# A ring of four instead of eight buffers for gathered expert v rows

## The chip, the cores and the metric

One core of a Trainium2 chip runs the whole program. The metric is the device time of one execution in microseconds. The kernel before took 5160.54 us (median of three runs, 5151.05 to 5163.83). TensorE is called PE here, VectorE DVE, ScalarE ACT, GpSimd POOL and SyncE SP, as in the profile.

## The reference, cut to what matters

Two layers of a diffusion backbone work on 5 blocks of 128 tokens with 1024 channels. Each layer has attention and pooling, and then the part that this case is about, a mixer that fetches expert rows by key:

```
def one_block(xb):                        # 128 tokens
    q = (xb @ wq).reshape(n, 8, 2, 64)
    s = einsum('nhpk,pmk->nhpm', q, sub_keys)
    sv, si = top_k(s, 16)                 # best 16 of 128 keys, on both sides
    ...                                   # best 16 of the 256 pairs: expert numbers e, gates g
    act = gelu(einsum('nd,nhkd->nhk', xb, u[e]))
    return einsum('nhk,nhkd->nd', g * act, v[e])
```

So every token has 8 heads with 16 experts each, and every expert costs one row of `u` and one row of `v`, each 1024 float32 numbers (4 KB). For the 128 tokens of a block one such step is a transfer of 512 KB.

## The kernel before

Five engines run lists of instructions written out by hand, with semaphores between them. A layer has two stages: attention with its projections, and the expert stage, which takes about 72% of the span.

The expert stage runs over *units*. A unit is one block (5) and one head (8): 40 units in a layer, 80 in all; they are counted from 0 to 79 here (`unit` in the code), and rows within a unit from 0 to 15. u5 of a unit is its sixth u row, v4 its fifth v row. For each unit:

- DVE finds the 16 experts of every token (`topk`, in short steps put between other work, two units ahead).
- POOL issues one indirect DMA for each row (`gather`, L578; POOL runs the list in order). Its loop takes, for k from 0 to 15, row k of u of the *next* unit and then row k of v of *this* unit. Before an issue it waits until the buffer is free: `used >= row - n + 1`, n being the number of buffers of the ring. The u ring has 4 buffers (`URING`), the v ring 8 (`RING`).
- DVE takes the dot product of each u row with the tokens (L1221, in the order of landing). A second instruction reads the sum out and frees the buffer.
- When all 16 are done, ACT applies gelu (L830). DVE multiplies by the gates (`weights`, L1194), but only behind the dot product of row 0 of the next unit. ACT then makes 16 diagonal matrices of the weights (L837).
- PE multiplies each diagonal with its v row and adds it up in PSUM (`v_rows`, L1564; four matmul records for each row, two halves of 512 columns in two passes). The last of them frees the v buffer (`v_used`).

PE and ACT do other things between the v rows of two units. `BESIDE` puts, behind the v rows of units 0 to 4 of each layer, queries for later blocks and gate rows there (L1533, L812). Before the v rows of the last unit of a block, PE also turns the tokens of the next block (`peer_tokens`, L1555), and before each unit it computes scores (L1549). At a block's end ACT copies the sum (L851) and DVE adds it to the tokens.

The tile `PR` is used twice. In the attention stage it holds queries, keys and values (13312 floats for each partition); in the expert stage it holds the v ring from its start, and behind the ring the queries `pq_T`.

Of the kernel before, what the change touches and what calls it, by code (L numbers as in the profile page):

```python
# [15 lines left out]
P = 128  # L16
D = 1024
KC = D // P
LAYERS = 2
NB = 5  # L20
# [12 lines left out]
PH, NKEYS, TOPK = 8, 128, 16  # L33
NEXP = NKEYS * NKEYS
NEG = -1e30
URING, RING = 4, 8
SPAN = 3 * STRIP
RB = (2 * WIN_R - 1) * (2 * WIN_C - 1)
RB_PAD = 64
# [85 lines left out]
def build(nc, x_prompt, x_sample, c, c_ctx, cache_nat_k, cache_nat_v, cache_mla_ckv, cache_mla_krope,  # L125
# [6 lines left out]
    with ExitStack() as ctx:  # L132
        def sb(name, free, dt=f32, parts=P):
            return ctx.enter_context(nc.sbuf_tensor(name, [parts, free], dt))
# [10 lines left out]
        HO = sb("h_or_mixed", NB * D)  # L145
        WR = sb("weight_ring", SLOTS * KC * 512)
        QKN = sb("na_qk_or_gates", 3 * NB * P + 3 * NKB * P)
        PR = sb("mla_qkv_or_expert_rows", RING * D + PH * NB * P)
        SC = sb("scratch", 4608)
        GB = sb("bias_or_small_weights", 2304)  # L150
        rows = sb("vec_rows", P)
# [45 lines left out]
        o = 0  # L197
        qm_T = PR[0:QK, o:o + HEADS * NB * P].rearrange("p (h t) -> p h t", h=HEADS)
        o += HEADS * NB * P
        km_T = PR[0:QK, o:o + HEADS * NKB * P].rearrange("p (h t) -> p h t", h=HEADS)  # L200
        o += HEADS * NKB * P
        v_mla = PR[:, o:o + NKB * WIDTH].rearrange("p (b h e) -> p b h e", b=NKB, h=HEADS)
        o += NKB * WIDTH
        v_na = PR[:, o:o + NKB * WIDTH].rearrange("p (b n) -> p b n", b=NKB)
        o += NKB * WIDTH
        mod_rows = PR[0:2, 0:2 * 512].rearrange("p (s n) -> p s n", s=2)
        lat_T = PR[:, o:o + 256].rearrange("p (k t) -> p k t", k=2)
        v_ring = [PR[:, i * D:(i + 1) * D] for i in range(RING)]
# [1462 lines left out]
```

## Time and profile before

| | |
|---|---|
| median of three runs | 5160.54 us |
| the profiled execution | 5150.62 us, its span 5148.8 us |
| PE busy | 3930.9 us (76%) |
| POOL busy | 2554.3 us (50%) |
| DVE busy | 2559.4 us (50%) |
| ACT busy | 946.7 us (18%) |
| gathers | 2560, with 1342 MB of the 1448 MB that are moved |
| granted PE clock, mean | 0.926 |

The page of the profile gives the busy time of each engine, a strip of the span in 40 slices, a chain of work that ended last, and groups of instructions. The expert stages are slices 6 to 20 and 26 to 40, where the DMA engines are busy for nine tenths. POOL's busy time is the making of the gathers; the time in which the data moves is in the DMA rows.

### The profile page before, as it was taken

To read this page: it belongs to the slowest core of one execution; us is meant where nothing else is said; L and a number is where in the kernel's file an instruction comes from. 1 tells how busy PE (TensorE), PEld (TensorE's weight loads), DVE (VectorE), ACT (ScalarE), POOL (GpSimd) and SP (SyncE) were. 2 spreads that over 40 slices of the span, in tenths; PEclk is the share of its full clock that TensorE was granted. 3 is DMA by queue.
4 is the path that set the end of the run, shared out by engine and by line. 5 is a ranking of instruction groups with operands and counts; after the bars stand their busy time and mean duration, and the time that the engine had idled before them with its cause. 6 is when DMAs were issued, how large, how long until landed. Compare 5 with 4: busy or idle time off the path is not lost. (4 is left out here: it accounts for less than half of the span.)

```text
span 5148.8 us, 36114 instructions
## 1 busy us (share of the span) xinstructions
PE 3930.9 (76%) x10138; PEld 1745.8 (34%) x10138; DVE 2559.4 (50%) x6404; ACT 946.7 (18%) x2474; POOL 2554.3 (50%) x2831
## 2 busy tenths in 40 slices
PE   7889958777777677777788898688776777776777
PEld 3467333322222222222244664333222222222222
DVE  1243155455665556565422431555656565565563
ACT  1132112111111111111111321111111111111111
POOL 1210045566666666666612000455666666666665
PEclk9985989999999999999999859899999999999999
DMA  4110268899999999999930102688999999999998
GB/s 160 40 59 17 98 244 306 324 389 363 374 359 366 362 369 364 364 370 364 368 109 35 59 33 98 237 329 322 371 369 366 363 367 369 364 370 359 373 367 332
DMA packets 435149, 1448.27 MB, mean 281 GB/s; under 512 B 59236, under 2 KB 69768, under 8 KB 434440
## 3 DMA queue, kind: packets, MB, share of 16 engines
q0 software_dynamic: 368640, 1342.34, 68.7%
q1 hardware_dynamic: 66312, 103.61, 5.9%
q8 instruction: 86, 1.41, 0.1%
q14 instruction: 111, 0.91, 0.0%
HBM read 1442.20 MB, written 3.57 MB: 281 GB/s over the span
## 5 line engine op out<-in xcount | busy, mean ns | idle before, releaser
L1564 PE MATMUL scores<-mla_qkv_or_expert_rows,weight_diagonals 128*128 128x512 f32 x5120 | 2574.6, 634 | 1039.3 <-DMA mla_qkv_or_expert_rows<-in_peer_v,experts 587.6
L1564 PEld LDWEIGHTS scores<-mla_qkv_or_expert_rows,weight_diagonals 128*128 128x128 f32 x5120 | 925.7, 197 | 2653.5 <-issue 2436.2
L578 POOL DMA_INDIRECT mla_qkv_or_expert_rows<-in_peer_v,experts x1280 | 1209.5, 945 | 642.6 <-issue 368.7
L1221 DVE CUSTOM_DVE_ANT_0 bias_or_small_weights<-bias_or_small_weights,scores_transposes 128x1024 f32<-128x1024 f32 x640 | 779.3, 1218 | 529.2 <-DMA bias_or_small_weights<-in_peer_u,experts 443.6
L1221 DVE CUSTOM_DVE_ANT_0 na_qk_or_gates<-na_qk_or_gates,scores_transposes 128x1024 f32<-128x1024 f32 x640 | 779.5, 1218 | 475.7 <-DMA na_qk_or_gates<-in_peer_u,experts 332.1
L578 POOL DMA_INDIRECT na_qk_or_gates<-in_peer_u,experts x640 | 604.2, 944 | 535.8 <-DVE dots L1221 257.3
L578 POOL DMA_INDIRECT bias_or_small_weights<-in_peer_u,experts x640 | 608.9, 951 | 253.3 <-issue 173.9
L521 POOL TENSOR_SCALAR stat_biased<-stat_sums 128x6 f32<-128x6 f32 (+1 forms) x82 | 16.3, 199 | 1107.0 <-ACT scratch L607 823.0
L837 ACT ACTIVATE weight_diagonals<-ident,expert_weights 128x128 f32<-128x128 f32 x1280 | 386.7, 389 | 306.4 <-DVE expert_weights L1194 112.4
L1342 PE MATMUL products<-weight_ring,h_or_mixed 128*128 128x384 f32 (+2 forms) x800 | 266.4, 494 | 0.0
L819 ACT ACTIVATE scratch<-scratch 128x16 f32<-128x16 f32 x80 | 24.7, 308 | 1245.4 <-issue 550.8
L1262 PE MATMUL scores_transposes<-ident,scratch 128*128 128x128 f32 (+1 forms) x814 | 166.0, 340 | 100.0 <-POOL scratch L544 34.9
L830 ACT ACTIVATE gelu_dots<-dots 128x16 f32<-128x16 f32 x80 | 17.3, 217 | 1064.7 <-issue 671.6
L1342 PEld LDWEIGHTS products<-weight_ring,h_or_mixed 128*128 128x128 f32 x800 | 153.7, 206 | 99.6 <-issue 43.7
L1262 PEld LDWEIGHTS scores_transposes<-ident,scratch 128*128 128x128 f32 (+1 forms) x814 | 116.8, 169 | 145.6 <-issue 58.0
L1289 PE MATMUL products<-weight_ring,silu_cond 128*2 128x512 f32 x320 | 147.1, 617 | 11.4 <-DMA weight_ring<-in_w_mod 11.4
L939 DVE COPY scratch<-scores_transposes 128x256 f32<-128x256 f32 x80 | 33.7, 422 | 233.2 <-remote 191.5
L1485 PE MATMUL products<-mla_qkv_or_expert_rows,scratch 128*128 128x64 f32 x864 | 147.1, 327 | 0.0
L1533 PE MATMUL products<-h_or_mixed,weight_ring 128*128 128x128 f32 (+1 forms) x512 | 144.1, 444 | 3.3 <-issue 3.3
L1485 PEld LDWEIGHTS products<-mla_qkv_or_expert_rows,scratch 128*128 128x128 f32 x864 | 145.6, 252 | 0.5 <-issue 0.4
L1517 PE MATMUL products<-weight_ring,scratch 128*128 128x512 f32 x320 | 144.4, 611 | 0.0
L1221 DVE DVE_READ_ACCUMULATOR2_ANT dots<- 128x1 f32 x1280 | 106.8, 83 | 0.6 <-issue 0.6
(176 smaller groups left out, 2712.5 us busy)
## 6 DMA issues: line engine op xcount, KB each, us to landing
weight_ring<-in_w_mod SPq DMA_DIRECT2D x24, 2048.0 KB, 8.6
mla_qkv_or_expert_rows<-in_peer_v,experts POOLq DMA_INDIRECT x1280
na_qk_or_gates<-in_peer_u,experts POOLq DMA_INDIRECT x640
bias_or_small_weights<-in_peer_u,experts POOLq DMA_INDIRECT x640
weight_ring<-in_w_in SPq DMA_DIRECT2D x6, 1536.0 KB, 6.9
weight_ring<-in_t_pool SPq DMA_DIRECT2D x4, 2048.0 KB, 7.6
weight_ring<-in_w_out SPq DMA_DIRECT2D x4, 2048.0 KB, 7.8
weight_ring<-in_peer_wq SPq DMA_DIRECT2D x4, 2048.0 KB, 8.0
```

The source lines that it names most:

```text
L578: g.indirect_dma_start(ring[row % n], None, table, bass.IndirectOffsetOnAxis(ap=idx_st[:, col:col + 1], axis=0),).then_inc(row_in[row % n] ...
L819: a_.activation(tk["ex"], tk["tv"], ACT.Exp, bias=tk["nmx"], accum_out=tk["sum"]).then_inc(gexp_ready, 1)
L837: a_.activation(diags[:, k * P:(k + 1) * P], ident[:, :], ACT.Copy, scale=wgt[:, w:w + 1]).then_inc(diag_ready, 1)
L939: v_.tensor_copy(tk["scores"], key_scores(unit)).then_inc(score_free, 1)
L1221: v_.tensor_tensor_reduce(out=u_ring[at % URING], in0=u_ring[at % URING], in1=tokens, scale=1.0, scalar=0.0, op0=ALU.mult, op1=ALU.add, ac ...
L1262: ins = t_.transpose(dst[0:n, j * P:(j + 1) * P], v, ident[:, :])
L1289: ins = t_.matmul(dst[0:2, :], sct[:, :].rearrange("p (c k) -> p k c", c=2)[:, kk, :], w[:, kk, :], start=kk == 0, stop=kk == KC - 1)
L1342: ins = t_.matmul(dst[:, 0:n], hT(b, kk), w[:, kk, 0:n], start=kk == 0, stop=kk == KC - 1)
L1485: ins = t_.matmul(dst[:, h * DH:(h + 1) * DH], prob_T[(i - 2) % 2][:, k, :], val, start=k == 0, stop=k == len(blocks) - 1)
L1517: ins = t_.matmul(dst, o_T[ots.slot((l, b))][:, kk, :], w[:, kk, :], start=kk == 0, stop=kk == KC - 1)
L1533: ins = t_.matmul(dst[:, 0:(b1 - b0) * P], w[:, kk, (h % 4) * P:(h % 4 + 1) * P], h_blocks[:, b0:b1, kk, :], start=kk == 0, stop=kk == KC - 1)
L1564: ins = t_.matmul(acc[:, hf * 512:(hf + 1) * 512], diags[:, k * P:(k + 1) * P], v_ring[at % RING][:, hf * 512:(hf + 1) * 512], start=n % P ...
```

## The change

The ring of v rows gets four buffers. The constant `RING` sets the number of buffers, of semaphores `v_row_in`, and the distance of POOL's wait: gather of v row r now waits until row r-4 has been used, not r-8. The ring of u rows and the order of the gathers stay. The tile `PR` keeps its 13312 floats; the queries `pq_T` now begin behind four rows instead of eight, and as the view takes all of the rest of the tile, the queries of two heads lie 1152 floats apart instead of 640.

```
-URING, RING = 4, 8
+URING, RING = 4, 4
...
-        PR = sb("mla_qkv_or_expert_rows", RING * D + PH * NB * P)
+        PR = sb("mla_qkv_or_expert_rows", 13312)
```

## Rows read from the trace of the kernel before

**Rows 1.** The page: DMA strip, rate of its 40 slices, chain by engine.

```profile
DMA  4110268899999999999930102688999999999998
GB/s 160 40 59 17 98 244 306 324 389 363 374 359 366 362 369 364 364 370 364 368 109 35 59 33 98 237 329 322 371 369 366 363 367 369 364 370 359 373 367 332
...
PE 13%; POOL 12%; issue 8%; DMA 7%; another core or an unknown queue 3%; DVE 2%; ACT 0%; DVEq 0%; POOLq 0%; ACTq 0%
```

**Rows 2.** The page's groups: busy us, mean ns, idle before and what ended it.

```profile
L1564 PE MATMUL scores<-mla_qkv_or_expert_rows,weight_diagonals 128*128 128x512 f32 x5120 | 2574.6, 634 | 1039.3 <-DMA mla_qkv_or_expert_rows<-in_peer_v,experts 587.6
...
L578 POOL DMA_INDIRECT mla_qkv_or_expert_rows<-in_peer_v,experts x1280 | 1209.5, 945 | 642.6 <-issue 368.7
```

**Rows 3.** POOL, timeline, unit 20: start, us, [idle before, releaser]; v2, v3, v4.

```profile
1691.58 0.94 POOL L578 DMA_INDIRECT mla_qkv_or_expert_rows<-in_peer_v,experts  x1 [4.79 <-remote]
...
1694.07 0.94 POOL L578 DMA_INDIRECT mla_qkv_or_expert_rows<-in_peer_v,experts  x1 [0.30 <-issue]
...
1696.55 0.94 POOL L578 DMA_INDIRECT mla_qkv_or_expert_rows<-in_peer_v,experts  x1 [0.30 <-issue]
```

**Rows 4.** PE, timeline, unit 20: v0 with v1, then v2, v3, v4.

```profile
1691.80 3.70 PE L1564 MATMUL scores<-mla_qkv_or_expert_rows,weight_diagonals 128*128 128x512 f32 x8 [2.99 <-ACT weight_diagonals L837]
1696.11 1.96 PE L1564 MATMUL scores<-mla_qkv_or_expert_rows,weight_diagonals 128*128 128x512 f32 x4 [0.61 <-DMA mla_qkv_or_expert_rows<-in_peer_v,experts]
1699.93 1.95 PE L1564 MATMUL scores<-mla_qkv_or_expert_rows,weight_diagonals 128*128 128x512 f32 x4 [1.87 <-DMA mla_qkv_or_expert_rows<-in_peer_v,experts]
1703.01 1.96 PE L1564 MATMUL scores<-mla_qkv_or_expert_rows,weight_diagonals 128*128 128x512 f32 x4 [1.13 <-DMA mla_qkv_or_expert_rows<-in_peer_v,experts]
```

**Rows 5.** Waits of POOL, whole span: us in total, times, longest.

```profile
POOL na_qk_or_gates L578 <- DVE dots L1221: 257.3, 81, 13.1
```

**Rows 6.** POOL, timeline, unit 2: v0, v4, then u5 of the next unit.

```profile
816.06 0.94 POOL L578 DMA_INDIRECT mla_qkv_or_expert_rows<-in_peer_v,experts  x1 [2.06 <-remote]
...
826.03 0.94 POOL L578 DMA_INDIRECT mla_qkv_or_expert_rows<-in_peer_v,experts  x1 [0.30 <-issue]
837.08 0.94 POOL L578 DMA_INDIRECT na_qk_or_gates<-in_peer_u,experts  x1 [10.11 <-DVE dots L1221]
```

**Rows 7.** PE, timeline, unit 2: the queries before it, its first v rows.

```profile
818.99 13.90 PE L1533 MATMUL products<-h_or_mixed,weight_ring 128*128 128x512 f32 x32
...
835.82 14.41 PE L1564 MATMUL scores<-mla_qkv_or_expert_rows,weight_diagonals 128*128 128x512 f32 x29 [2.50 <-ACT weight_diagonals L837]
```

**Rows 8.** L1564 in stretches: PE and PEld busy (instructions), clock, DMA share, GB/s.

```profile
1100.30:1104.12 3.82, 3.81 (x5) 1.74 (x6) 0.50 0.93 341
835.80:838.79 2.99, 2.97 (x5) 1.38 (x6) 0.65 1.05 408
...
2430.80:2434.45 3.65, 3.65 (x5) 1.70 (x6) 0.54 0.58 173
3454.20:3457.52 3.32, 3.31 (x5) 1.50 (x6) 0.58 0.14 19
```

**Rows 9.** POOL, timeline, unit 43: v4, then u5 of the next unit.

```profile
3443.22 0.94 POOL L578 DMA_INDIRECT mla_qkv_or_expert_rows<-in_peer_v,experts  x1 [0.30 <-issue]
3455.46 0.94 POOL L578 DMA_INDIRECT na_qk_or_gates<-in_peer_u,experts  x1 [11.30 <-DVE dots L1221]
```

**Rows 10.** PE, timeline, unit 43: its first v rows.

```profile
3454.21 10.12 PE L1564 MATMUL scores<-mla_qkv_or_expert_rows,weight_diagonals 128*128 128x512 f32 x19 [2.50 <-ACT weight_diagonals L837]
```

**Rows 11.** POOL, timeline, unit 7: v4.

```profile
1101.25 0.94 POOL L578 DMA_INDIRECT mla_qkv_or_expert_rows<-in_peer_v,experts  x1 [0.30 <-issue]
```

**Rows 12.** POOL, timeline, unit 36: v4.

```profile
2433.10 0.94 POOL L578 DMA_INDIRECT mla_qkv_or_expert_rows<-in_peer_v,experts  x1 [0.30 <-issue]
```

**Rows 13.** All engines in two stretches: us, PE, PEld, DVE, ACT, POOL, clock, DMA, GB/s.

```profile
680.00:1060.00 380.00, 279.69 (x598) 111.57 (x596) 202.83 (x551) 62.54 (x160) 207.73 (x220) 0.91 0.86 322
1060.00:2560.00 1500.00, 1082.24 (x2193) 394.89 (x2194) 890.53 (x2264) 256.78 (x673) 988.71 (x1047) 0.96 0.96 367
```

**Rows 14.** PE, timeline, unit 79: v4 to v15.

```profile
5121.29 20.84 PE L1564 MATMUL scores<-mla_qkv_or_expert_rows,weight_diagonals 128*128 128x512 f32 x48 [0.73 <-DMA mla_qkv_or_expert_rows<-in_peer_v,experts]
```

## The prediction, made before the changed kernel was run

> **What bounds the kernel now.** I read the page first. Its DMA strip and rates show the two expert stages, flat at about 365 GB/s with the DMA engines nine tenths busy; the chain that ended last names no single engine, but mostly PE, POOL and DMA [rows 1]. The change touches only the v rows, so the groups come next: PE spends 2574.6 us on 1280 v rows, 2.01 us each, and stood idle for 587.6 us because a v row had not landed; making a gather costs POOL 0.945 us [rows 2].
>
> The pace is in the timelines. POOL issues one gather in 1.245 us (0.94 of work, 0.30 of gap): v3 at 1694.07 and v4 at 1696.55 have one u gather between them, so a pair of u and v takes 2.49 us [rows 3]. PE needs 1.96 us of these for a v row, and it waits for the DMA before v2, v3 and v4 [rows 4]. So within a unit POOL's list sets the pace, and whatever holds POOL up holds up both rings. Three things hold it: pauses of 2 to 5 us every 28 gathers or so, which the trace puts down to no engine (4.79 us before v2, [rows 3]; I count 94, of 3.8 us); the u ring (257.3 us in 81 waits on one of its two tiles, the longest 13.1 us, [rows 5]); and, in no case, the v ring: going through all 1280 v gathers, none was issued less than 3.3 us after the row eight before it was used.
>
> So the question is by how much a ring of four would have bound. I set each issue of v row r beside the end of PE's fourth matmul on row r-4, and split what I found by the place in the unit.
>
> **Within a unit: nothing.** v4 of unit 20 is issued at 1696.55 and PE starts on it at 1703.01, 6.46 us later, because of the DMA [rows 3, 4]. With 1.96 us of matmuls and the 0.3 us that POOL takes to go on, a buffer is taken for 8.7 us. Four buffers allow one row every 8.7 / 4 = 2.2 us, and POOL asks for one every 2.49 us. The margin is 9.96 - 8.7 = 1.2 us. Cost 0, if the landing doesn't take longer than now. That it would take less, with fewer gathers under way, seems more likely, since a stall lets the queue run empty.
>
> **At the start of a unit: four kinds.** v4 waits for v0, and v0 can't be used before the unit's gelu, weights and first diagonal are there. In unit 20 v0 and v1 are done at 1695.5, v0 alone about 1693.8, and v4 went out at 1696.55 [rows 3, 4]: covered, by POOL's pause.
>
> (a) Behind the work of `BESIDE`, 10 units (1 to 5 and 41 to 45). PE computes queries for 13.90 us, and unit 2's v0 starts only at 835.82 [rows 7]; its four matmuls end at about 838.8 [rows 8]. v4 had gone out at 826.03 [rows 6], so it would be 13 us late. But POOL stood still anyway: the next gather, u5, came at 837.08 after 10.11 us of waiting for DVE [rows 6]. What counts is how much later u5 comes: 838.8 + 0.27 for v4, + 1.25 for u5 = 840.3, 3.2 us later. Unit 43 the same way: v0 starts at 3454.21 and ends at about 3457.5, u5 at 3455.46, so 3457.5 + 1.52 - 3455.46 = 3.6 us [rows 8 to 10]. The ten lie between 1.8 and 3.8 us and sum to 29 us. The stall is longer than any queue of gathers, so nothing hides it: 29 us on the path.
>
> (b) The last unit of a block, 7 units (7, 15, 23, 31, 55, 63, 71). Here PE turns the next block's tokens first. In unit 7 v0 starts at 1100.30 and ends near 1104.1, as PE has just stood idle and its four matmuls run at a granted clock of 0.50, which is 1.2 GHz [rows 8]. v4 was issued at 1101.25 [rows 11]: 1104.1 + 0.27 - 1101.25 = 3.1 us late. The seven sum to 22 us.
>
> (c) 22 other units in which v0 is late by chance, such as unit 36: v0 ends at 2434.4, v4 was issued at 2433.10, 1.6 us late [rows 8, 12]. Between 0.1 and 2.7 us each, 16 us in all. In the 39 units left over (the last of each layer is apart, below), a ring of four would not have been waited for.
>
> (d) The last unit of each layer has no u gathers. PE alone sets its end: it takes v4 to v15 in 20.84 us, 1.74 us each [rows 14], so four rows in 7.0 us. With a ring of four, a buffer turns round in 0.3 + 1.96 us and the time from issue to PE's start: 4.53 us for v2 of unit 20, which was issued after a pause, or 6.46 us for v4 [rows 3, 4]. That is 6.8 or 8.7 us, and costs twelve rows 0 or 12 x 1.7 / 4 = 5 us. Few gathers are under way there, so I stay near the lower end: 1.5 us in each layer, 3 us.
>
> A stall in (b) and (c) begins with about five gathers under way (6.46 us at 1.245), and the DMA works on. After a pause a v row needs 4.53 us, two rows later 6.46 us [rows 3, 4], so up to 1.9 us of a stall can be hidden at first; but as the latency grows back within some gathers, a part is paid after all. I take half: 19 us of 38. Bounds: 38 with nothing hidden, 0 with all of it.
>
> The rest has one answer. `pq_T` with 1152 floats between heads has the same operands of each instruction in form, so ACT L812 and PE L1549 cost what they did; four semaphores fewer cost or give nothing; `PR` is as large. No DMA is added or moved past another. Behind POOL's new wait stand only gathers, first u5 of the next unit, for which DVE waits. A gain could come only from rows that land sooner once fewer are under way; the sum leaves it out, and I bound it at 10 us, one microsecond in each unit of (a).
>
> **Sum.** 29 + 19 + 3 = 51 us. The profiled execution took 5150.62 us, 9.9 below the median of 5160.54. So 5202 for an execution like the profiled one, and 5160.5 + 51 = 5211.5 against the median, which I predict as 5211.
>
> **The rivals.**
>
> *The stalls are hidden (not slower).* If the DMA, not POOL, set the pace over a longer stretch, then POOL's pauses would be its slack: what the v ring delays, the next pause would give back. Place: POOL's pauses, 94 of 3.8 us; it decides if a pause shrinks by what came late before. Then (b) and (c) are 0, and (a) keeps a part, 0 to 20 us: 5160 to 5180, typically 5165. For it: 9 tenths of DMA share. Against it: the stretch with the BESIDE units moves 322 GB/s and the rest 367 [rows 13]; a stall isn't made up for there, and the pauses are as frequent in it. The Trainium skill bears on this rival (HBM Reference, Specifications): it gives a core about 358 GB/s as its share, and says that one that streams alone measures more. By the share alone the gathers' 1342 MB would take 3750 us, about the length of both stages, and the change would cost nothing; the 367 GB/s of [rows 13] are above it, and so the trace disagrees with the share as a limit here.
>
> *The ring binds in every pair (much slower).* If the landing takes over 1.2 us longer than the 6.46 us, each pair costs (cycle)/4 and not 2.49 us. At 0.1 us for each of 1280 pairs that is 128 us more: 5340. For it: the margin is thin, and next-layer weights under way beside gathers lengthen landings. Against it: a ring that stalls has fewer rows under way, and these land sooner.
>
> *Faster.* Four rows fewer under way shorten the wait for u rows at the start of a unit, by up to 0.3 us in each of 80 units or 24 us, and the stalls are hidden too: 5140. Nothing in the trace shows it.
>
> **Chances.** Forecast (25 to 90 us later) 0.70; hidden 0.14; binding in every pair 0.12; faster 0.04. A difference below 0.3%, 15.5 us, can't be told from none. Of the hidden case three quarters fall within it: faster 0.03, same 0.13, slower 0.84. The range takes in the full 70 us and some of the two neighbours: 5168 to 5270.
>
> **What would show it.** In the profile after, POOL should wait for PE before v4 in some 35 to 40 units; in the ten BESIDE units the wait of 10 us moves from u5 (on DVE) to v4 (on PE), and u5 follows 1.25 us behind v4. POOL's waits for DVE fall by about 100 us and those for PE rise by 150. Within units the pace stays 2.49 us. PE's and DVE's busy time stay the same within 1%. The rate falls by 1% in the flat slices. I am wrong if v8 to v15 wait for PE in many units (the ring binds), or if POOL's pauses got shorter or fewer (hidden).

## The result

The changed kernel took 5208.16 us (median of four runs, 5202.75 to 5214.84) against 5159.91 us: 48 us more, a ratio of 1.0097 with a 95% interval of 1.0079 to 1.0114. I had said 5211 us, 51 us more. The profiled execution is the slowest of the four, 5214.84 us with a span of 5213.0 us; 64 us more than the profiled one of before.

The page of the kernel after, with the lines that answer to [rows 1, 2]:

```profile
DMA  4110267799999999999931102677999999999998
GB/s 158 40 58 33 97 230 283 300 372 368 367 341 370 373 352 368 373 349 369 367 125 40 58 33 97 230 290 298 367 369 372 365 368 368 361 372 368 373 368 323
...
L1564 PE MATMUL scores<-mla_qkv_or_expert_rows,weight_diagonals 128*128 128x512 f32 x5120 | 2572.3, 631 | 1108.5 <-DMA mla_qkv_or_expert_rows<-in_peer_v,experts 753.2
...
L578 POOL DMA_INDIRECT mla_qkv_or_expert_rows<-in_peer_v,experts x1280 | 1209.1, 945 | 999.1 <-PE scores L1564 411.1
```

The work is what it was (2572.3 us of PE for the v rows, 1209.1 us of POOL for their gathers). POOL's idle time before v gathers rose from 642.6 to 999.1 us, and the largest part of it is now put down to PE. The loss is not even over the stage: slices 7 and 8 fell from 306 and 324 GB/s to 283 and 300, slices 27 and 28 from 329 and 322 to 290 and 298, while the flat slices of the second layer are mostly within 1%; in the first layer slices 9, 12, 15 and 18 lost 4 to 6% as well. The same in stretches (columns as in [rows 13]):

```profile
680.00:1060.00 380.00, 269.02 (x564) 105.94 (x563) 191.22 (x517) 56.33 (x142) 194.31 (x207) 0.90 0.80 297
1060.00:2560.00 1500.00, 1059.55 (x2166) 382.58 (x2165) 885.75 (x2261) 260.42 (x688) 978.12 (x1034) 0.97 0.96 364
```

322 GB/s became 297 in the stretch with the BESIDE units, 8% less; 367 became 364 in the rest, 1% less. POOL's waits answer to [rows 5] (us in total, times, longest):

```profile
POOL mla_qkv_or_expert_rows L578 <- PE scores L1564: 411.1, 178, 19.1
...
POOL na_qk_or_gates L578 <- DVE dots L1221: 54.2, 51, 7.8
```

The wait for DVE on this u tile went from 257.3 to 54.2 us. (Most of the 143.9 us that the profile of before puts down to PE for v rows are pauses that it can't name: set beside the end of the matmuls, POOL waited 0.6 us for v buffers before and 241 us after.) The wait moved from the u ring to the v ring, as forecast, but it got longer than forecast. The timeline of POOL in unit 3 shows how; first the kernel before (v0, then u5 of the next unit), then the kernel after (v0, v4, u5, v13):

```profile
871.04 0.95 POOL L578 DMA_INDIRECT mla_qkv_or_expert_rows<-in_peer_v,experts  x1 [5.64 <-issue]
...
891.62 0.94 POOL L578 DMA_INDIRECT na_qk_or_gates<-in_peer_u,experts  x1 [9.67 <-DVE dots L1221]
```

```profile
877.62 0.95 POOL L578 DMA_INDIRECT mla_qkv_or_expert_rows<-in_peer_v,experts  x1 [0.30 <-issue]
...
906.41 0.94 POOL L578 DMA_INDIRECT mla_qkv_or_expert_rows<-in_peer_v,experts  x1 [19.13 <-PE scores L1564]
907.66 0.94 POOL L578 DMA_INDIRECT na_qk_or_gates<-in_peer_u,experts  x1 [0.30 <-DVE dots L1221]
...
931.88 0.94 POOL L578 DMA_INDIRECT mla_qkv_or_expert_rows<-in_peer_v,experts  x1 [3.38 <-remote]
```

Before, POOL's unexplained pause (5.64 us) fell ahead of the wait for the queries. It cost nothing there: without it POOL would have come to u5 earlier and waited longer. After, the pause (3.38 us) falls on v13, behind the wait, where all that follows is late. I summed this over the ten units behind BESIDE work, from every gather of both traces. Pauses ahead of the long wait were 31.6 us before and 5.3 us after, pauses behind it 2.0 us before and 28.3 us after. The ten units took 546.4 us from v0 to the next v0 before and 604.3 us after, 58 us more; the seven last units of blocks 338.9 and 341.3 us; 59 others 2690.4 and 2694.8 us.

So the total came out as forecast, but not its parts: 29 us had been given to the ten units, which lost 58, and 19 to the others, which lost 7. Part of the agreement is luck. One pair of traces can't tell whether this split is the mechanism or chance, and that was the question of the experiments. Several kernels of them keep eight buffers and shorten only the distance of POOL's wait, so that the place of the stall can be chosen.

### The profile page after: what moved, and what is told of

It reads as the page before. It is cut to its first block and busy times, and to the rows that moved or that the text cites. A ratio compares the mean times of both kernels' runs of the same rounds, so it can differ in the third digit from the quotient of the medians.

```text
span 5213.0 us, 36114 instructions
## 1 busy us (share of the span) xinstructions
PE 3927.5 (75%) x10138; PEld 1729.6 (33%) x10138; DVE 2569.2 (49%) x6404; ACT 942.1 (18%) x2474; POOL 2557.1 (49%) x2831
## 5 line engine op out<-in xcount | busy, mean ns | idle before, releaser
L1564 PE MATMUL scores<-mla_qkv_or_expert_rows,weight_diagonals 128*128 128x512 f32 x5120 | 2572.3, 631 | 1108.5 <-DMA mla_qkv_or_expert_rows<-in_peer_v,experts 753.2
L1564 PEld LDWEIGHTS scores<-mla_qkv_or_expert_rows,weight_diagonals 128*128 128x128 f32 x5120 | 910.7, 196 | 2736.5 <-issue 2543.0
L578 POOL DMA_INDIRECT mla_qkv_or_expert_rows<-in_peer_v,experts x1280 | 1209.1, 945 | 999.1 <-PE scores L1564 411.1
L1194 DVE TENSOR_TENSOR expert_weights<-gelu_dots,gates 128x16 f32<-128x16 f32 x80 | 13.8, 173 | 184.2 <-ACT gelu_dots L830 168.6
```

The costliest lines, as they stand in the source:

```text
L578: g.indirect_dma_start(ring[row % n], None, table, bass.IndirectOffsetOnAxis(ap=idx_st[:, col:col + 1], axis=0),).then_inc(row_in[row % n] ...
L1564: ins = t_.matmul(acc[:, hf * 512:(hf + 1) * 512], diags[:, k * P:(k + 1) * P], v_ring[at % RING][:, hf * 512:(hf + 1) * 512], start=n % P ...
```

## The experiments

Each is compared with the kernel before on the same chip. The chips differ, and that turned out to matter: on two of them the kernel before takes 4861 to 4862 us, and the traces taken there hardly show a pause of POOL; on two others it takes 5153 and 5174 us, and the traces are full of them. The kernel before was traced only on the first chip and on one without pauses.

**The wait alone, everywhere.** In `gather`:

```
+                    if ring is v_ring:
+                        n = 4
                     if row >= n:
                         pool.wait_ge(used, row - n + 1)
+                    n = len(ring)
```

> Eight v buffers and the layout of before, but POOL waits for the v row four before, as after the change. If the wait alone makes the difference (theory): +48 us against before, as the changed kernel, within 10 us. If the layout of the queries or the smaller number of buffers and semaphores has a part (rival): less than +35 us.

4917.26 us against 4862.01, ratio 1.0113 (1.0096 to 1.0129), +55 us. The wait is the whole of the change. The changed kernel itself, on another chip without pauses, gave nearly the same:

> The changed kernel. With few pauses (time of before about 4860 us): +55 us, as with eight buffers and a distance of four (+55), if the number of buffers and the layout of the queries cost nothing; 29 to 33 us of it in the ten units behind the queries. With many pauses (5160 us): +48 us.

4917.71 against 4861.22 us, ratio 1.0117 (1.0100 to 1.0133), +56 us. Four real buffers, fewer semaphores and the other layout of the queries add nothing to the distance that these intervals (8 us to either side) could show.

**Only behind the queries, and only elsewhere.**

```
-                        n = 4
+                        n = 4 if unit % UNITS in (1, 2, 3, 4, 5) else 8
```

> Eight buffers; the distance of four only for the v rows of units 1 to 5 and 41 to 45, behind the queries; eight elsewhere. The trace of the changed kernel shows these ten units 58 us longer in sum and all others only 5 us. Theory (those ten units carry nearly all): +40 to +58 us. Rival, the sum of the prediction (29 us from these ten, the rest from units spread over the stage): +25 to +32 us.

4893.21 against 4862.01 us, ratio 1.0062 (1.0045 to 1.0079), +31 us.

```
-                        n = 4
+                        n = 8 if unit % UNITS in (1, 2, 3, 4, 5) else 4
```

> The complement of the run before it: distance four everywhere but in those ten units. Theory: the rest is hidden by POOL's pauses, 0 to +8 us. Rival, the sum of the prediction: +19 to +22 us, up to +41 us if nothing is hidden.

4887.64 against 4862.01 us, ratio 1.0054 (1.0038 to 1.0071), +26 us. The two add up (31 + 26 = 57 against 55). The theory that I had taken from the trace of after, nearly all in the ten units, missed both; here the parts are those of the prediction, 29 and 19, with the second somewhat larger.

**One gather in each of the ten units.**

```
-                        n = 4
+                        n = 4 if k == 4 and unit % UNITS in (1, 2, 3, 4, 5) else 8
```

> Eight buffers, and a single gather in each of the ten units, v4, waits for the row four before it, v0; all others have the distance of eight. If the start of the unit is the place: the same as with the distance of four for all rows of the ten units, within 8 us. If rows v5 to v15 bind as well (their wait for v1 to v11, or the pause that moved into them comes from these waits): at least 15 us less than that.

4890.92 against 4862.01 us, ratio 1.0057 (1.0040 to 1.0073), +29 us: within 2 us of the distance four for all rows of these units, with intervals of 8 us. The wait of v4 for v0 is the place.

**The kernel before, for its trace.**

> The kernel before, for its trace beside the three that follow. The d4 kernels ran in about 4890 us where the kernel before takes 4862 us, not 5160 us, and their traces show 5 to 50 pauses of POOL instead of 94. If that is the chip and not the kernels: where this run takes about 4860 us, its trace has fewer than 20 pauses; where it takes about 5160 us, some 90.

4860.37 us. The rates of its page, to be held against [rows 1], and below it POOL's longest groups of waits in the changed kernel on the same chip:

```profile
GB/s 169 43 62 1 104 146 343 323 359 405 409 399 409 407 398 409 407 401 409 401 103 43 62 1 104 175 345 320 366 409 401 403 410 405 403 406 406 403 407 347
```

```profile
POOL mla_qkv_or_expert_rows L578 <- PE scores L1564: 491.8, 584, 18.2
POOL mla_qkv_or_expert_rows L578 <- issue: 227.2, 696, 2.8
```

The flat slices move 398 to 410 GB/s instead of 365. I find 5 pauses in it with 9 us in all, where the profiled execution of before had 94 with 356 us; that is about the difference of 300 us between the chips. In the two traces of this chip the ten units took 550.6 and 580.0 us (+29.4), the other units of the comparison 20.7 us more. The 550.6 us stand beside 546.4 us in the trace of before, which has the pauses: in these ten units the pauses cost the kernel before nothing, so they were hidden there. Hardly a pause stands behind the stall that could move. POOL in the changed kernel on this chip, unit 2, v4, u5 of the next unit, v13:

```profile
839.51 0.94 POOL L578 DMA_INDIRECT mla_qkv_or_expert_rows<-in_peer_v,experts  x1 [17.25 <-PE scores L1564]
840.75 0.93 POOL L578 DMA_INDIRECT na_qk_or_gates<-in_peer_u,experts  x1 [0.30 <-issue]
...
861.86 0.94 POOL L578 DMA_INDIRECT mla_qkv_or_expert_rows<-in_peer_v,experts  x1 [0.30 <-issue]
```

u5 goes out 1.24 us behind v4, and v13 without a pause. These two traces have every landing marked, so their pages give the median from issue to landing of the v rows, first with eight buffers, then with four:

```profile
mla_qkv_or_expert_rows<-in_peer_v,experts POOLq DMA_INDIRECT x1280, 8.5
```

```profile
mla_qkv_or_expert_rows<-in_peer_v,experts POOLq DMA_INDIRECT x1280, 7.5
```

A turn of a buffer (landing, matmuls of 1.96 us, 0.3 us to go on) takes about 10.8 us with eight buffers. Four buffers at 2.49 us give 9.96 us, so here the ring of four does bind within units; but as it binds, rows land sooner and the turn falls to 9.8 us, just inside.

**The same two again, on a chip with pauses.** These settle what the pair of traces left open.

> Again the distance of four in the ten units behind queries alone. The three chips so far differ in POOL's pauses: a kernel of before that takes 4860 us has hardly any, one that takes 5150 to 5160 us some 90 to 110. Without pauses: +31 us as the first time, within 5 us. With pauses, if they move from ahead of the ring's stall, where they were hidden, into the gathers behind it, as the trace of the changed kernel shows: +40 to +58 us; if that shift is chance: +25 to +35 us.

5226.94 against 5174.02 us, ratio 1.0102 (1.0086 to 1.0117), +53 us, where it was +31 without pauses.

> Again the complement. Without pauses: +26 us as the first time, within 5 us. With pauses, if they give back what the ring delays in these units: -3 to +8 us; if they don't: +19 to +26 us.

5187.08 against 5174.02 us, ratio 1.0023 (1.0013 to 1.0033), +13 us, where it was +26: between what the two expectations said. POOL in the first of them, unit 3, v4, u5, v13, as in the kernel after:

```profile
906.03 0.94 POOL L581 DMA_INDIRECT mla_qkv_or_expert_rows<-in_peer_v,experts  x1 [18.63 <-PE scores L1567]
907.28 0.94 POOL L581 DMA_INDIRECT na_qk_or_gates<-in_peer_u,experts  x1 [0.30 <-DVE dots L1224]
...
931.75 0.94 POOL L581 DMA_INDIRECT mla_qkv_or_expert_rows<-in_peer_v,experts  x1 [3.63 <-remote]
```

The pause is on v13 again. Over the ten units 1.5 us of pauses stand ahead of the long wait and 28.7 us behind it, on another chip and with eight buffers. So the shift isn't chance: with pauses, the stall of the v ring costs its own 3 us and a pause that was hidden before. Elsewhere the distance of four costs about half of what it costs without pauses, but the pauses don't give it back: outside the ten units, gaps of over 1 us for which no buffer was waited for make up 334 us before and 374 us after, and on this chip 322 us (distance eight there) and 396 us (distance four). What fell is POOL's wait for u rows, from 94 to 19 us and from 122 to 22 us, while it now waited 47 and 52 us for v rows. Why the sum comes out at half stays open.

**Five and three buffers.** `RING` is 5 or 3, and the queries stay where they were (`pq_T = PR[:, 8 * D:]`).

> v ring of five, queries where they were. Row v5 now waits for v0, one pair (2.49 us) later than v4 did. Theory (lateness of v0 against POOL's list): what was 3.2 us late in a unit is 0.7 us late: ten units behind queries 8 us, the last units of blocks 5 us, the rest near 0: +5 to +16 us against before. Rival, the loss follows the number of rows under way: a quarter less than the +55 us of four, +35 to +45 us.

5157.78 against 5152.57 us, ratio 1.0012 (1.0002 to 1.0022), +5 us. One buffer more than four brings back almost everything, as the lateness of v0 says (3.2 us, and a pair is 2.49 us); a loss by the number of rows under way was put at 35 to 45 us. The parts are less sure than the total. In this trace too the pauses of the ten units lie behind POOL's long wait (31 us behind it, 11 us ahead), and these units took 570.8 us, 24 us more than in the trace of before, while the seven last units of blocks took 324.2 us, 15 us less. Without a trace of the kernel before on this chip it stays open if the pauses move for another reason than the v ring's stall.

> v ring of three. Row v3 waits for v0, and a buffer turns round in 8.7 us if the landing takes what it took. Rival (a fixed latency): every pair takes 8.7 / 3 = 2.9 us instead of 2.49: 1280 x 0.41 = +520 us and 30 us more from the ten units. Theory (with fewer rows under way a row lands sooner, down to the 4.5 us seen after a pause, so that a turn takes 6.7 to 8.7 us): +150 to +400 us, and the median time from issue to landing of v rows falls from 6.2 us to between 5 and 5.8 us.

5308.92 us in one run against 5152.57: +156 us, at the lower end of the theory and far from 520. POOL's groups of gathers in v rows (mean ns, idle before):

```profile
L578 POOL DMA_INDIRECT mla_qkv_or_expert_rows<-in_peer_v,experts x1280 | 1203.7, 940 | 1125.7 <-PE scores L1564 637.9 <-issue 421.0 <-remote 66.5
```

POOL waited 610 us for v buffers by my count of each gather, and lost a quarter of that. Against the ring of five on the same chip, the pauses fell from 114 with 387 us to 53 with 111 us, and POOL's waits for u rows from 199 to 26 us. The median time from issue to landing of a v row fell as well, from 5.9 to 5.3 us, so that the waits for v rows are shorter than they would be with 5.9 (estimated from the DMA packets, as these traces don't mark all landings).

**Queries inside the unit, with eight and with four buffers.** PE does the two pieces of BESIDE work of a unit behind its v3 and v11; ACT's order stays.

```
                         ins.then_inc(v_used, 1)
+                        if k in (3, 11) and len(BESIDE.get(n, [])) > k // 8:
+                            use = BESIDE[n][k // 8]
+                            if use[0] == "q":
+                                queries(*use[1:])
...
                     v_rows(n)
-                    for use in BESIDE.get(n, []):
-                        if use[0] == "q":
-                            queries(*use[1:])
...
```

> Eight buffers, and the two pieces of BESIDE work of a unit are done behind v3 and v11 on PE instead of both behind v15; ACT takes their results behind its diagonals as before. The ten units no longer start behind 13.9 us of queries. Theory: POOL's wait of 9 to 13 us in each goes, and PE becomes their limit (16 x 2.0 + 13.9 + 0.6 = 47 us instead of 54.6): -60 to -75 us against before. Rival: the wait only moves into the unit, less than -25 us.

4754.86 against 4861.22 us, ratio 0.9781 (0.9765 to 0.9798), 106 us faster than the kernel before and the fastest of all. The ten units took 444.2 us instead of 550.6. I had counted 2.0 us for each v row of PE; queued up they take less. PE in unit 2, where the two pieces are gate rows:

```profile
816.99 6.17 PE L1323 MATMUL products<-weight_ring,silu_cond 128*128 128x512 f32 x14
823.00 13.90 PE L1564 MATMUL scores<-mla_qkv_or_expert_rows,weight_diagonals 128*128 128x512 f32 x32
836.73 1.02 PE L1323 MATMUL products<-weight_ring,silu_cond 128*128 128x512 f32 x2
```

Eight v rows in 13.90 us are 1.74 us each, so a unit needs 16 x 1.74 + 13.9 + 0.6 = 42 us of PE, not 47.

> The same order with the ring of four. Theory: a query of 7 us in the middle of the v rows outlasts what four buffers hide (1.2 us of margin), twice in each of the ten units, so POOL loses up to 5.8 us twice: +3 to +6 us in each against eight buffers, plus the 20 to 27 us of the other units: 50 to 85 us above the same order with eight buffers. Rival, only the start of a unit binds: 20 to 30 us above it.

4860.43 against 4861.22 us, ratio 0.9996 (0.9987 to 1.0006): 106 us slower than with eight buffers. With four buffers all of the gain is gone. The ten units took 503.8 us (+60), units 0 and 40, which now have queries too, 20 us more, and the others 22 us more. PE (the piece behind v3, then v4) and POOL (v8) in unit 2:

```profile
834.00 6.17 PE L1323 MATMUL products<-weight_ring,silu_cond 128*128 128x512 f32 x14
840.01 8.32 PE L1564 MATMUL scores<-mla_qkv_or_expert_rows,weight_diagonals 128*128 128x512 f32 x19
```

```profile
842.16 0.94 POOL L578 DMA_INDIRECT mla_qkv_or_expert_rows<-in_peer_v,experts  x1 [7.30 <-PE scores L1564]
```

v4's matmuls begin at 840.01 and its buffer is free at 841.9; v8 goes out 0.3 us later, after 7.30 us of waiting. With eight buffers, v8 waits for v0, which is long done.

## Why the prediction came out right, point by point

**Within a unit, cost 0.** Nearly held where it was made, on a chip with pauses: the median from issue to landing of v rows, estimated from the packets, is 6.0 us before and 5.9 after, and 193 of the 241 us that POOL waited for v buffers are before v4. Without pauses it did not hold: the landing of 8.5 us takes the whole margin of 1.2 us, and in the trace of four buffers two fifths of the v gathers (502 of 1280) go out 0.27 us after their buffer is free, most after a wait of 0.1 us or so. The reason given against the rival, that rows land sooner once the ring stalls, is shown there: 7.5 us. The statement that no v gather of the kernel before went out less than 3.3 us after its buffer was free leaves out the last unit of each layer; in unit 39 two of them waited, 0.6 us together.

**(a) The ten units, 29 us.** The mechanism is shown (one gather in each is enough, +29) and the size as well where POOL doesn't pause: +31 us timed, 29.4 in the traces. (7 of the 29.4 lie in unit 5 alone, where weights of the next layer are fetched beside the gathers; the other nine lost 2.5 us each, which is within the 1.8 to 3.8 of the forecast.) With pauses it was +53 timed and 58 in the traces. The step that failed is "the stall is longer than any queue of gathers, so nothing hides it: 29 us on the path". It asked what hides the new stall. It did not ask what the old stall at u5 had been hiding, and that was a pause of POOL in most of the ten units, 31.6 us in all ([rows 6] has one of 2.06 us ahead of v0 of unit 2).

**(b) and (c), 38 us at first, half of it hidden, 19.** Timed +26 us without pauses and +13 with them; 20.7 and 7 us in the traces. Half was a choice in the middle, and the two kinds of chip lie on both sides of it. The reason given for it, that the queue of gathers hides the first part of a stall, was tested by no run. The split within was off: in the traces without pauses the seven last units of blocks lost 3 us and not 11, as no clock of 0.50 was met by v0 of unit 7 there (its four matmuls took 1.98 us, not 3.8), and the others 18 us and not 8. A recount of v4 in the trace of before finds 14 units of kind (c) with 14 us, not 22 with 16.

**(d) The last units, 3 us.** From the issue of v0 to the last v row it was 36.8 us after and 35.4 before in unit 79, and 38.8 after and 35.2 before in unit 39: 5 us together, of which the stage that follows unit 39 made up 2. Without pauses it was 2 us.

**The sum.** 51 us forecast, 48 measured. On the chips with pauses there are two errors of opposite sign, which do not cancel: 24 to 29 us too few in (a), for pauses that moved into the path, and 6 to 12 us too many in (b) and (c). By parts the loss there is 64 us in the pair of traces, of which the executions that were profiled explain 16, being the fastest of before and the slowest of after. But it is 66 us timed as well (53 + 13, on another chip), where the medians of the first chip are 48 us apart (41 to 59 by the interval). What makes up this difference is not known, so that 51 met 48 so closely is in part luck. Without pauses the same sum is right to within 6 us (51 against 55 and 56), and so is (a); the rest is larger than forecast by some 7 us timed and 2 us in the traces, and is spread otherwise.

**The rivals.** "The stalls are hidden" is half true in its price outside the ten units on chips with pauses, but not in its mechanism: the pauses there got no shorter. With three buffers they did. Its price in (a) had the wrong sign: pauses made the loss larger. "The ring binds in every pair" is false at four buffers on the chip where the forecast was made, partly true at four without pauses, and mostly true at three (878 of 1280 v gathers go out 0.27 us after their buffer is free); and even there a row lands sooner and the time rises by 156 us and not by what a fixed latency gives. The Trainium skill gives a core about 358 GB/s as its share of the memory (HBM Reference, Specifications), and says that a core streaming alone measures more. The kernel with eight buffers moves 398 to 410 GB/s in the flat slices on a chip without pauses, so the trace disagrees with the share as a limit for this core and agrees with the second statement.

**What was to be seen.** u5 goes out 1.25 us behind v4, as said. POOL's wait for DVE fell by 203 us on one u tile (said: 100 in all), and that for PE rose by 267 us (said: 150), as the stall of the v ring begins a gather earlier and lasts 13 to 19 us. A wait before v4 of more than 0.3 us for its buffer is in 28 units, fewer than the 35 to 40 that I gave; without pauses it is in 60.

## What to carry to other kernels

A ring costs nothing while its turn (issue, landing, use) is shorter than the issue pace times the buffers, and it costs at the places where its first row has to wait; what counts there is how much later the first item behind the stall goes out, and comparing the issue time of row n with the time when row 0 is used gave it here before any run, where POOL did not pause. Ask of a stall that moves what it has been hiding, since a hidden pause may come into the path. And where a ring's stall is caused by a long piece of other work between two batches, dividing that work was worth twice the ring here, but only with buffers enough to cover each piece.

## What the runs showed of the hardware

POOL's pauses go with the chip, or with something else that went on there at the time, and not with the kernel alone. The same kernel before had 94 of them with 356 us in one trace and 5 with 9 us in another, and ran 300 us faster there. Where they occur and the ring of four stalled POOL behind the queries, the next one came 18 gathers behind the stall in nine of the ten units (eight of ten in the repeat with eight buffers), some 3.1 us beyond the usual gap of 0.3 us. In the changed kernel's trace all of them are before v gathers, in that of the kernel before about a third before u gathers. With three buffers they became rarer and shorter. They end when mostly two gathers are still under way (61 of the 101 over 2 us before, 97 of 119 after, with the landings estimated from the packets). What they are remains open: no engine of this core ends them in the trace, and no run took them away by itself.

A gather's time from issue to landing falls when a ring's stall holds back the number under way: from 8.5 us in the median with eight v buffers to 7.5 us with four on a chip without pauses, where the landings are marked. With pauses it is estimated from the packets, which comes out too short where the 16 DMA engines drift apart (6.3 us for the 8.5): about 6.0 us with eight, 5.9 with four, 5.3 with three.
